# A hybrid decoder trunk on one core: the residual of the expert stage moves from the router's stage to the last quad of each layer

## The reference, cut to what matters

```python
for layer in range(DEPTH):                       # DEPTH = 4
    mixed = mixer[layer % 3](x, ...)
    x = layer_norm(DEEPNORM_ALPHA * x + mixed, ln_mix_g[layer], ln_mix_b[layer])
    ffn = hierarchical_moe(x, ...)               # 32 experts of 1024 -> 256 -> 1024, top 2 in the top group
    x = layer_norm(DEEPNORM_ALPHA * x + ffn, ln_ffn_g[layer], ln_ffn_b[layer])
```

## Time and profile before

| | |
|---|---|
| median of 3 runs | 1414.23 us (1412.38 to 1414.73) |
| the profiled execution's own time | 1413.54 us |
| its span, first to last instruction | 1411.7 us, so 1.84 us lie around it |
| TensorE's mean granted clock | 0.990 of full speed |
| busy | PE 90%, PEld 48%, DVE 33%, ACT 22%, POOL 7% of the span |
| moved from HBM | 482.85 MB, 343 GB/s over the span |

### The profile page before, as it was taken

How to read it: one execution, slowest core, us unless ns; L and a number is a source line. 1 busy time by engine, 2 the same in 40 slices (tenths; PEclk the granted TensorE clock), 3 DMA queues, 4 the chain that set the end, 5 groups by cost and what they waited for, 6 DMA issues and landing times.

```text
span 1411.7 us, 18117 instructions
## 1 busy us (share of the span) xinstructions
PE 1268.0 (90%) x7422; PEld 683.5 (48%) x7422; DVE 463.9 (33%) x1014; ACT 306.4 (22%) x759; POOL 101.2 (7%) x184
## 2 busy tenths in 40 slices
PE   8999998878999999888889999889789999888875
PEld 7855534333574765333334666343338765543431
DVE  1456301102634884111017654110114455211103
ACT  1132312112222323222112103221112151221210
POOL 2221000000000620000000000000002030000000
PEclk9999999999999999999899999999999999999998
DMA  9756899999935139999999849999999447899995
GB/s 313 302 219 247 339 429 427 427 427 424 382 119 187 53 133 402 427 428 428 428 426 411 361 165 364 429 428 427 428 427 389 153 179 313 353 428 426 428 427 246
DMA packets 37671, 485.21 MB, mean 344 GB/s; under 512 B 4513, under 2 KB 4833, under 8 KB 7761
## 3 DMA queue, kind: packets, MB, share of 16 engines
q1 hardware_dynamic: 35424, 478.15, 82.1%
q0 software_dynamic: 2016, 5.36, 1.3%
q10 hardware_dynamic: 144, 0.47, 0.1%
HBM read 482.85 MB, written 1.05 MB: 343 GB/s over the span
## 4 chain that ended last, share of the span: by engine, by line
PE 73%; DMA 14%; DVE 7%; ACT 3%; issue 2%; POOL 0%; SPq 0%; DVEq 0%
PE psum L1166 13%; PE psum L848 12%; PE psum L879 11%; DMA memory<-in_units 10%; PE psum L1126 8%; PE psum L1206 7%; PE psum L1198 6%; PE psum L905 6%; DMA ring<-in_units 4%; ACT memory L1335 2%; DVE memory L2148 1%; PE psum L811 1%; PE psum L1291 1%; PE psum L805 1%; ACT memory L1541 1%
## 5 line engine op out<-in xcount | busy, mean ns | idle before, releaser
L848 PE MATMUL psum<-memory,ring 128*128 128x256 f32 x768 | 168.2, 381 | 0.3 <-DMA ring<-in_units 0.2
L2143 DVE TENSOR_TENSOR memory<-memory,psum 128x256 f32<-128x256 f32 x32 | 13.5, 421 | 463.3 <-ACT memory L1529 463.3
L1126 PE MATMUL psum<-memory,x 128*128 128x128 f32 x1024 | 132.4, 284 | 35.7 <-ACT memory L1335 35.0
L1206 PE MATMUL psum<-memory 128*128 128x512 f32 x240 | 119.1, 619 | 42.8 <-DVE memory L2148 22.8
L1126 PEld LDWEIGHTS psum<-memory,x 128*128 128x128 f32 x1024 | 121.0, 194 | 74.0 <-issue 69.9
L848 PEld LDWEIGHTS psum<-memory,ring 128*128 128x128 f32 x768 | 146.0, 191 | 21.8 <-issue 2.0
L1166 PE MATMUL psum<-ring,memory 128*32 128x512 f32 x1152 | 137.9, 615 | 17.6 <-DMA ring<-in_units 17.5
L1335 ACT ACTIVATE memory<-psum,affine_t 128x128 f32<-128x128 f32 x312 | 117.4, 457 | 139.3 <-PE psum L1126 132.7
L879 PE MATMUL psum<-ring,memory 128*128 128x512 f32 x280 | 122.8, 594 | 0.9 <-ACT memory L1335 0.9
L1166 PE MATMUL psum<-memory 128*32 128x512 f32 x896 | 103.3, 598 | 3.2 <-DMA memory<-in_units 3.2
L1206 PEld LDWEIGHTS psum<-memory 128*128 128x128 f32 x240 | 40.7, 189 | 124.0 <-DVE memory L2148 48.6
(11 more groups left out here) (246 smaller groups left out, 1297.6 us busy)
## 6 DMA issues: line engine op xcount, KB each, us to landing
ring<-in_units SPq DMA_DIRECT2D x129, 2048.0 KB, 25.7
memory<-in_units SPq DMA_DIRECT2D x88, 2048.0 KB, 23.5
memory<-in_units SPq DMA_DIRECT2D x16, 1024.0 KB, 26.5
ring<-in_units SPq DMA_DIRECT2D x4, 512.0 KB, 9.5
memory<-in_ln_ffn_g POOLq DMA_DIRECT2D x4, 512.0 KB, 11.5
memory<-in_ln_ffn_b POOLq DMA_DIRECT2D x4, 512.0 KB, 17.1
memory<-in_const SPq DMA_DIRECT2D x3, 456.0 KB, 33.5
x<-in_x SPq DMA_DIRECT2D x2, 512.0 KB, 4.9
```

Source lines behind the costliest of these rows:

```text
L848: last = nc.tensor.matmul(bank(key, T, s * T), w[:, 2 * m + s, k, :], xT[:, k, :], start=(k == 0), stop=(k == KD - 1))
L1126: last = nc.tensor.matmul(psum[:, to, (at + i) * P:(at + i + 1) * P], x[:, c, k * P:(k + 1) * P], sel[:, par, c, :], start=(c == 0), stop= ...
L1206: last = nc.tensor.matmul(psum[:, 4 + NH * c + h, :], hT[:, FC + c, :], y_sb[:, h * HB:(h + 1) * HB], start=False, stop=last_quad, skip_gr ...
```

## The change

The residual's matmuls leave the router's stage. In the last quad, PE transposes x again, four blocks before each gate and up unit (`late_transposes`, bank 1). ACT drains each four into a free early slot, scaled by alpha times g and b (`late_drains`). PE adds them with the identity into banks 4 to 7 (`late_residual`), before the next unit. The fillers of the last quad go. In the router's stage fillers stand where the residual was, and the wait on bank 2 (`free(("rank", l))`) moves ahead of the logits of chunk 0. The first half of the last slot's load waits for the logits. The first quad's combine now begins the banks. DVE makes the table `late_affine` in one small instruction. The table of alpha times the identity is gone from the constants.

```diff
-        "alpha": np.eye(P) * ALPHA,
-EARLY_AT = 4944
+EARLY_AT = 5072
+        late_xT = {k: region(work, EARLY_AT + s * UNIT, [KD, T]) for k, s in {0: 3, 1: 0, 2: 2}.items()}
+        late_affine = region(small, 176, [2, KD])
@@ SP, first_load
-                    sp.wait_ge(residual_made, l + 1)
+                    sp.wait_ge(*filled(("logits", l)))
@@ PE
+            def late_transposes(l, part):
+                half, c = HALVES[part]
+                for i in range(4):
+                    k = 4 * half + i
+                    last = nc.tensor.transpose(psum[:, 1, i * P:(i + 1) * P], x[:, c, k * P:(k + 1) * P], ident)
+                last.then_inc(late_filled, 1)
+            def late_residual(l, part):
+                half, c = HALVES[part]
+                pe.wait_ge(late_drained, 4 * l + part + 1)
+                for i in range(4):
+                    nc.tensor.matmul(psum[:, 4 + NH * c + half, i * P:(i + 1) * P], late_xT[KINDS[l]][:, 4 * half + i, c * P:(c + 1) * P], ident,
+                                     start=False, stop=False, skip_group_check=True)
@@ PE, quad
-                    if u and last_quad and sems is first:
-                        pe.wait_ge(sems["xw_ready"], n * 2 + (2 + FREE))
-                        keep_busy(2, 1)
+                    if last_quad and sems is first:
+                        if u == 0:
+                            pe.wait_ge(sems["xw_ready"], n * 2 + (2 + FREE))
+                        else:
+                            late_residual(n // NQ, u - 1)
+                        late_transposes(n // NQ, u)
...
+                if last_quad and sems is first:
+                    late_residual(n // NQ, GU - 1)
                 pe.wait_ge(sems["hT_ready"], n + 1)
...
-                                                start=False, stop=last_quad, skip_group_check=True)
+                                                start=first_quad, stop=last_quad, skip_group_check=True)
@@ PE, the router's stage
                 free(("logits", l))
+                free(("rank", l))
                 for c in range(TC):
                     if c:
                         free(("xT", 2 * l, c, 0))
                         keep_busy(1, FILLS.bank["xT", 2 * l, c, 0])
                         for half in range(2):
                             x_transposes(2 * l, c, half)
-                        free(("rank", l))
                         keep_busy(1, FILLS.bank["rank", l], 2)
...
-                    last = residual([c])
-                last.then_inc(residual_made, 1)
-                keep_busy(1, FILLS.bank["xT", 2 * l, 1, 0])
+                        keep_busy(3, FILLS.bank["xT", 2 * l, 1, 0])
+                    else:
+                        keep_busy(2, FILLS.bank["rank", l])
@@ ACT, at the head of the last quad
+            def late_drains(l):
+                act.wait_ge(late_scaled, l + 1)
+                for part, (half, c) in enumerate(HALVES):
+                    act.wait_ge(late_filled, 4 * l + part + 1)
+                    for i in range(4):
+                        k = 4 * half + i
+                        ins = nc.scalar.activation(late_xT[KINDS[l]][:, k, c * P:(c + 1) * P], psum[:, 1, i * P:(i + 1) * P], ACT.Identity,
+                                                   scale=late_affine[:, 0, k:k + 1], bias=late_affine[:, 1, k:k + 1])
+                    ins.then_inc(late_drained, 1)
@@ DVE, gate_values
+                v.tensor_scalar(late_affine, affine_t[:, 2 * l, :, :], ALPHA, None, ALU.mult).then_inc(late_scaled, 1)
```

More of the change, by code:

```diff
@@ L338, in build @@
         ln_eps = table("eps")
-        alpha_i, causal, iota, rev, join = (table(n) for n in ("alpha", "causal", "iota", "rev", "join"))
+        causal, iota, rev, join = (table(n) for n in ("causal", "iota", "rev", "join"))
         def region(t, at, shape):
@@ L473, in build @@
         ones_set = sem("ones_set")
-        residual_made = sem("residual_made")
         dve_step, act_step = sem("dve_step"), sem("act_step")
@@ L482, in build @@
         rows_in, carried = sem("rows_in"), sem("carried")
+        late_scaled, late_filled, late_drained = sem("late_scaled"), sem("late_filled"), sem("late_drained")
         fg_ready, log_ready = sem("fg_ready"), sem("log_ready")
@@ L1524, in first_tokens @@
                 token_blocks(l, 0, (2, 3), 2).then_inc(first["xw_ready"], 1)
+            def late_drains(l):
[7 more added lines that the diff above has]
+                    ins.then_inc(late_drained, 1)
             def quad(l, sems, n, par, ahead, by_columns=False):
+                if by_columns:
+                    late_drains(l)
                 act.wait_ge(sems["unit_used"], n * QU + (GU + spare(sems)))
```

## The result

The changed kernel took 1430.12 us (median of 4 runs, 1426.78 to 1434.34), the kernel before, timed beside it, 1414.48 us (1412.38 to 1415.54). The ratio is 1.0105 with a 95% interval of 1.0091 to 1.0120: slower, as forecast, but by 15.6 us where the prediction had 3.1, and above its range (1414.3 to 1420.5). The profiled execution is the slowest of the four, 1434.34 us.

The account below looks back on a forecast made before the run. Weight transfers bound the expert stage, whose end follows unit 12's issue. Three layers at 0.85 us plus layer 1 at 0.85 - 0.3 gave +3.1 us: 1416.6 us, or 1417.3 us against the median; range 1414.3 to 1420.5 us.

Parts of the forecast that it names:

- the scope of the sum: Expert stage ends a constant after unit 12's issue, so only PE's delay before unit 0 counts; mixers untouched, at no cost.
- The wait on bank 2: Router's stage: first logits wait for DVE's whole drain, delaying transposes and unit 12; 0.81 to 0.90 us a layer, residual-to-filler swap included.
- the rival of the free wait: Router's stage: slack before the transposes hides most of the wait; +0.8 us in all, 1415.0 us; chance 0.14.
- Residual to fillers: Router's stage: two fillers (1.92 us) in place of the residual's 16 records (1.87 us), +0.05 us a layer.
- the three fillers behind the second logits: Router's stage: three fillers (2.9 us) replace residual and filler (2.9 us), end before DVE's L2101 and cost nothing.
- The earlier issue of the last slot's first half: Last slot's load: its first half goes out about 1 us earlier, but nothing comes of it.
- The last quad: End of expert stage: pieces of 1.41 us replace 1.92, PE reaches unit 3 1.06 us earlier; layers 0, 2, 3 gain nothing.
- layer 1 giving back: Layer 1's last quad, where PE itself is behind: up to 0.58 us can be won, 0.3 us taken.
- ACT's drains covered: Last quad: ACT's four drains (1.50 us) hide behind the unit's own matmuls (1.86 us).
- the cheaper last quad: Rival: PE bounds the layers' ends and gains 0.9 us a layer; 1410.6 us with no router loss; chance 0.07.
- The falling clock: Rival: PE's clock halves in the last quad after a longer wait, +3 to +4 us in layer 3; about 1421 us; chance 0.12.

Follow-up runs that it names:

- thirteenth kernel: Changed kernel whole, with PE's expert code starting at places 16, 251, 16, 16 of its 256-instruction block in layers 0 to 3: 1421.45 us, ratio 1.0048.
- twelfth kernel: Changed kernel with the wait on bank 2 put back and expert code at places 16, 251, 16, 16 in layers 0 to 3: 1416.79 us, ratio 1.0016.
- second kernel: Changed kernel with the wait on bank 2 put back and the fillers behind the first logits in another bank: 1424.60 us, ratio 1.0063.
- fourth kernel: Kernel before with only its expert code's starting place moved from 68 to 141: 1428.64 us, ratio 1.0086.
- first kernel: Changed kernel with its expert code's starting place moved from 68 to 251: 1436.22 us, ratio 1.0146.
- fifth: Changed kernel with its expert code's starting place moved from 68 to 16: 1429.62 us, ratio 1.0112.
- ninth kernel: Changed kernel with the wait on bank 2 put back and expert code at place 16, but 130 in layer 2: 1424.11 us, ratio 1.0056.
- tenth: Changed kernel with the wait on bank 2 put back and expert code at place 16, but 68 in layer 2: 1419.52 us, ratio 1.0025.
- seventh kernel: Kernel before with only the wait on bank 2 moved ahead of the first logits, the residual left where it was: 1419.38 us, ratio 1.0035.
- eighth: Changed kernel with expert code at place 16 and one filler added ahead of the wait on bank 2: 1426.17 us, ratio 1.0085.
- third kernel: Changed kernel with expert code at place 251 and the wait on bank 2 put back: 1431.00 us, ratio 1.0098.
- sixth: Changed kernel with expert code at place 16 and the wait on bank 2 put back: 1422.84 us, ratio 1.0056.

## Why the prediction was wrong, step by step

The 15.6 us part in three, by medians, each against the kernel before on the same chip: the place of the code 8.6 (15.6 less the 7.0 of the thirteenth kernel), the wait 4.7 (thirteenth less twelfth, 7.0 - 2.4), the residual in the last quad 2.4 (twelfth). Taken off in the other order, they give 6.4 for the place (second less twelfth, 8.8 - 2.4) and 6.9 for the wait (changed less second, 15.6 - 8.8). So place and wait together are some 13 us, and how that divides is known only to some 2 us.

- **The step that failed is the scope of the sum**: "what matters of this change is what it does to PE before unit 0. The mixers lie on PE and DVE, and the change touches nothing in them." It counted what the instructions do and not where they lie. 73 more of them moved a join in its block, and three gaps of 2.1 to 2.2 us with some 3.4 us of half clock behind each followed. What the prediction put at nothing cost 6.4 to 8.6 us by the medians. By the first row of the table, less 0.96 us of wait, layers 1 to 3 lost 2.3, 3.1 and 3.7 us, together 9.1; in the profile of the second kernel, which has no wait, they lost 8.7. Shown: a loss comes with a constant alone (fourth kernel), moves as the constant moves it (first, fifth, ninth and tenth), and goes with places chosen by the rule (twelfth, thirteenth). Not shown is how much of the price is the gap and how much the half clock behind it.
- **The wait on bank 2**, 0.81 to 0.90 us a layer: the mechanism was right, and so was the sum, in part by luck. The logits came 0.96 us later. But PE had some 0.14 us of slack ahead of the transposes: from logits to transposes it took 4.59 us before (858.28 - 853.69) and 4.45 after (874.21 - 869.76), and 4.51 in the seventh kernel, which keeps the residual behind the same wait. So the transposes came 0.82 us later where the clock stayed up, and of the rival of the free wait a small part was true. Not in the sum: PE's 0.80 us of idle time ahead of sixteen matmuls of 36 columns let the clock fall behind them, in two of four layers of this profile, for 1.5 us each (router row of the table). In the four profiles of versions with the wait ahead, fillers behind and no cover it fell in 2, 1, 2 and 1 of four layers (changed, first, fifth, thirteenth); with the idle time filled (eighth) in none of four, with the wait put back, in six profiles, in none of 24. The seventh kernel has the idle time and no fall, and still took 5.1 us in the median, where the delays of its logits add to some 3.6 (2.6 in layers 1 to 3 and, as an estimate, one more in layer 0); why is open.
- **Residual to fillers, +0.05 us**: -0.06 by the numbers above (4.45 - 4.51), as good as nothing. With the wait put back the router's stage took what it took before, so the three fillers behind the second logits cost nothing.
- **The earlier issue of the last slot's first half brings nothing**: unit 12's issue moved with PE's use of unit 0, 1.97 us behind its start in either kernel (168.15, 570.68). No run tested this term by itself.
- **The last quad**: pieces of 1.53 us (forecast 1.41), layer 1 giving back 0.39 us (forecast 0.3), ACT's drains covered. In the changed kernel PE waits for transfers in all four tails (2.71 us before unit 3 in layers 0 and 1, 2.08 before the first down unit in layer 2). Its price of 2.4 us in the twelfth kernel (0.8 to 3.8) was forecast as -0.3. The profile of that kernel shows +0.8 us of span; which step holds the rest the single profile doesn't tell.
- **The rivals.** The free wait is refuted but for 0.14 us a layer, the cheaper last quad by four tails that wait for transfers. The falling clock was there in layer 3; the estimate of +3 to +4 us was too high, since the transfers absorbed all but 0.6 us. The trace agrees only in part with what the prediction quotes from the Trainium skill ("TensorE: Matmul & The Clock Gate", "HAM oscillation — how this bites in real kernels"): the clock fell behind the wait of 3.32 us and not behind those of 2.71 us in layers 0 and 1. Nor does it take the missing fillers: in the fourth kernel it fell with them in place.
- **The start.** In the profile of the changed kernel the first logits of layer 0 came 4.7 us later beyond the wait; PE's first matmul with weights began at 11.66 us, 9.58 before. The fourth kernel, with the old code up to there, shows 3.5 us of it; of the second and third, which have the same code up to there, the third shows 4.9 and the second none. So it is a scatter of runs, not the change, and goes most of the way from the 15.6 us between medians to the 20.8 us between spans.

No version beat the kernel before by more than a measurement tells: the nearest are the kernel before at place 16 (0.9995, which is the same) and the residual in the last quad with places chosen (1.0016, slightly slower). The residual was no bound where it stood: with fillers in its place and the wait put back, the router's stage took 15.6 us as before.

## What to carry to other kernels

When a change adds or removes instructions in a long unrolled program with jumps, list where every jump and its target come to lie in their 256-instruction blocks, before and after, for the whole code behind the edit. A stall of PE with releaser "issue" and a packet of the instruction queue inside it, or a jump instruction of PE that takes thousands of ns in place of some 300, is the mark of this; the profile can also name an engine that had long been done. And test a surprising loss first with the place alone: one constant told more here than any piece of the change. A wait moved ahead of short matmuls costs its idle time and may cost the clock behind it; in the one profile with a filler in front of it the second part was gone.

## What the runs showed of the hardware

- PE stalled for its code in two ways. Where it landed close ahead of a block's end, it ran what was left and then stood: from the first instruction behind the jump to the first over the border there are 5.5 us (third kernel, 1220.28 to 1225.73) to 6.6 us (fourth, 349.47 to 356.10), 5.9 in the changed kernel (353.24 to 359.10). Where a jump led to a block that was not there, the jump itself took 5.8 us (eighth), 6.0 (fifth), 6.3 (sixth) and 6.7 (ninth), against at most 0.42 in the kernel before. In the sixth PE had by the count entered the block that it jumped from some 1.7 us earlier, so that "6 us from the entry" is rough. The queues of the weights ran full in these stretches; that they set the 6 us is not shown. Less is seen as a gap by what PE still has to run: 2.1 us behind fillers and three or four transposes, nothing behind 90 instructions.
- The Trainium skill ("Runtime: NRT & Kernel Launch", "Instruction fetch mechanics") says that each engine fetches its code in sequence in blocks of 256 instructions (16 KiB), mostly hidden, and that a taken branch out of the blocks at hand stalls. The traces agree on the branch (the ninth kernel's 6.7 us). That a crossing is hidden did not hold soon behind a jump: in the changed kernel PE had landed in the block without a stall and stood still at its end, 2.13 us.
- The gap at a place is not the same in each run: in the first kernel's profile, its fastest run (1425.77 us), layer 3 showed 0.92 us; in the third kernel the same place showed 4.97 us, and the first kernel's other runs took 1436 us.
